# Feed-forward of a two-model block: one 512-column matmul for the high and low data against the high weights

## The reference

```python
for l in range(DEPTH):                                  # DEPTH = 2
    h = rms_norm(x, attn_norm_g[l])
    ...                                                 # three mixers on h @ w_in[l]
    x = x + jnp.concatenate([ya, yb, yc], axis=-1) @ w_out[l]
    h = rms_norm(x, ffn_norm_g[l])
    x = x + (jax.nn.silu(h @ ffn_w_gate[l]) * (h @ ffn_w_up[l])) @ ffn_w_down[l]
return rms_norm(x, final_norm_g)
```

## Time and profile before

| | |
|---|---|
| time, median of 3 runs | 940.64 us |
| lowest and highest | 939.58 and 940.69 us |
| span of the profiled execution | 938.7 us |
| time of the median run outside such a span | 1.9 us |
| mean granted clock of TensorE over the span | 0.997 |
| first feed-forward stage, PE | 147.2 to 327.6 us |
| second feed-forward stage, PE | 460.9 to 641.2 us |

### The profile page before, as it was taken

One profiled execution on the slowest core, in us unless ns is written; L12 is line 12 of the kernel. 1 busy time (PEld: TensorE's weight loads), 2 busy tenths in 40 slices (PEclk: granted clock), 3 DMA queues, 4 the chain that ended last, 5 costly groups with the idle time before them and its releaser, 6 DMA issues.

```text
span 938.7 us, 20423 instructions
## 1 busy us (share of the span) xinstructions
PE 916.4 (98%) x8848; PEld 869.5 (93%) x8848; DVE 680.7 (73%) x972; ACT 555.8 (59%) x851; POOL 7.6 (1%) x12
## 2 busy tenths in 40 slices
PE   8899999999999999999999999999999999999996
PEld 7788799999999999878999999999989899989896
DVE  6899667866664589976777666448799679588675
ACT  6873566654443588355754544338587667585665
POOL 0010000000000001000000000000000000000000
PEclk9999999999999999999999999999999999999998
DMA  8342115665554544211466655554544335444231
GB/s 324 151 174 95 48 56 188 214 261 183 201 201 180 180 163 151 98 64 46 140 251 232 250 192 182 204 197 135 179 136 138 132 135 180 147 168 157 93 135 67
DMA packets 24169, 150.94 MB, mean 161 GB/s; under 512 B 2960, under 2 KB 3472, under 8 KB 7056
## 3 DMA queue, kind: packets, MB, share of 16 engines
q1 hardware_dynamic: 24080, 149.64, 44.7%
HBM read 147.26 MB, written 1.05 MB: 158 GB/s over the span
## 4 chain that ended last, share of the span: by engine, by line
PE 67%; DVE 20%; ACT 7%; issue 3%; SPq 1%; DMA 1%; DVEq 0%; ACTq 0%
PE bank L1914 9%; PE bank L1912 8%; PE bank L1913 8%; DVE w_lo L277 6%; PE bank L2145 4%; PE bank L1936 3%; PE bank L1934 3%; PE bank L1935 3%; PE bank L2146 3%; PE bank L2147 3%; ACT w_hi L271 2%; PE bank L1075 1%; PE bank L2177 1%; PE bank L589 1%; PE bank L1165 1%
## 5 line engine op out<-in xcount | busy, mean ns | idle before, releaser
L277 DVE TENSOR_TENSOR w_lo<-w_raw,w_hi 128x1024 fp32r<-128x1024 f32 x256 | 306.0, 1224 | 106.2 <-ACT w_hi L271 105.5
L271 ACT ACTIVATE w_hi<-w_raw 128x1024 fp32r<-128x1024 f32 x256 | 259.4, 1054 | 206.3 <-PE bank L1914 104.9
L1912 PE MATMUL bank<-act_hi,w_hi 128*128 128x256 f32 x704 | 194.5, 276 | 0.0
L1913 PE MATMUL bank<-act_lo,w_hi 128*128 128x256 f32 x704 | 194.3, 276 | 0.0
L1914 PE MATMUL bank<-act_hi,w_lo 128*128 128x256 f32 x704 | 194.3, 276 | 0.0
L1912 PEld LDWEIGHTS bank<-act_hi,w_hi 128*128 128x128 f32 x704 | 132.2, 188 | 0.1
L1913 PEld LDWEIGHTS bank<-act_lo,w_hi 128*128 128x128 f32 x704 | 132.2, 188 | 0.0
L1914 PEld LDWEIGHTS bank<-act_hi,w_lo 128*128 128x128 f32 x704 | 132.2, 188 | 0.0
L2145 PE MATMUL bank<-act_hi,w_hi 128*128 128x256 f32 x352 | 100.2, 285 | 0.3
L2147 PE MATMUL bank<-act_hi,w_lo 128*128 128x256 f32 x352 | 97.7, 278 | 0.0
L2146 PE MATMUL bank<-act_lo,w_hi 128*128 128x256 f32 x352 | 97.7, 278 | 0.0
(11 more groups left out here) (367 smaller groups left out, 1982.1 us busy)
## 6 DMA issues: line engine op xcount, KB each, us to landing
w_raw<-in_w_ffn SPq DMA_DIRECT2D x66, 1024.0 KB, 4.8
w_raw<-in_w_mix SPq DMA_DIRECT2D x62, 1024.0 KB, 4.9
small_w<-in_small SPq DMA_DIRECT2D x2, 1280.0 KB, 7.6
w_raw<-in_w_mix SPq DMA_DIRECT2D x8, 256.0 KB, 6.3
x_res<-in_x_channels SPq DMA_DIRECT2D x4, 256.0 KB, 6.1
probs<-in_w_mix SPq DMA_DIRECT2D x2, 512.0 KB, 7.5
probsT<-in_w_mix SPq DMA_DIRECT2D x1, 1024.0 KB, 10.1
mem<-in_mem_channels SPq DMA_DIRECT2D x1, 1024.0 KB, 7.2
```

What stands on the lines that cost most here:

```text
L271: self.nc.scalar.activation(hi, self.piece(self.raw_slot(g), p), ACT.Copy).then_inc(self.hi_ready, 1)
L277: self.nc.vector.tensor_tensor(lo, self.piece(self.raw_slot(g), p), hi.bitcast(fp32), ALU.subtract).then_inc(self.lo_ready, 1)
L1912: TE.matmul(o, hi[:, w], HI[:, k, :], start=(k == 0 and x == 0), stop=False)
L1913: TE.matmul(o, hi[:, w], LO[:, k, :], start=False, stop=False)
```

## The change

Gate and up chunks 6 to 21 and all down chunks get a new form. `HI` and `LO` become two halves of one tile `HL`, and `GHI` and `GLO` of `GHL`. The high weights meet both in one matmul of 512 columns, whose moving operand is 256 columns of the high and 256 of the low data. It fills a whole bank: half h = 0 holds high times high, half h = 1 holds high times low. The matmul of low weights and high data adds into half 1. An output tile thus takes a bank of its own, and its two halves are added when they are taken out: for gate and up, ACT copies half 1 of two banks (`gate_rest`, `up_rest`), DVE adds half 0 and multiplies by the norm's row in a second operation; for down, `x_add_halves` adds one half to `X` after the other. Chunks 0 to 5 keep the old form.

Since eight down outputs now take all eight banks, and the gate/up chunks still use some of them at first, the down weights are cut anew (`DOWN_TILES`): a first pass over all 22 k tiles for outputs 0 to 3, in banks 4 to 7, and a second for outputs 4 to 7, in banks 0 to 3. There are 16 blocks a chunk as before. The adds of the first four outputs stand in the middle of the down part, and at the stage's end the split of chunk N+1 moves ahead of `lo(3)`. Semaphore names of the final norm also change ("turned"), with no change to its work.

```diff
+DOWN_TILES = [(k, o) for h in (0, 4) for k, o in
+              [(k, h + x) for k in range(FK - 4) for x in range(4)] + [(k, h + x) for x in range(4) for k in range(FK - 4, FK)]]
...
-        self.HI = self.sb("act_hi", [P, KT, T], f32r)
-        self.LO = self.sb("act_lo", [P, KT, T], f32r)
+        self.HL = self.sb("act", [P, 2, KT, T], f32r)
+        self.HI, self.LO = self.HL[:, 0, :, :], self.HL[:, 1, :, :]
...
+        if self.down and p in (0, 3):
+            eng.wait_ge(self.K.st.chunk_used, self.chunk - (0 if p else 6))
+        elif self.down:
+            eng.wait_ge(self.K.sem("out_done"), 2 * (self.n - 1) + p)
+        elif p % 2:
             eng.wait_ge(self.K.st.chunk_used, self.chunk - 1 + p // 2)
         else:
             eng.wait_ge(self.K.sem("out_done"), 2 * (self.n - 1) + p // 2 + 1)
...
+    def x_add_halves(self, dve, ch, p, halves):
+        x = self.K.X[:, 2 * p:2 * p + 2, :]
+        self.wait_out(dve, p)
+        ch(self.nc.vector.tensor_tensor(x, x, halves[:, :, 0, :], ALU.add))
+        self.nc.vector.tensor_tensor(x, x, halves[:, :, 1, :], ALU.add).then_inc(self.K.sem("x_new"), 1)
...
+    def first_bank(i):
+        return (4, 6, 0, 2)[(i - WIDE) % 4]
+    def halves(n):
+        return K.PS[:, 512 * n:512 * (n + 2)].rearrange("p (j h t) -> p j h t", j=2, h=2)
...
+    def wide_part(pe, i, p):
...
         hi, lo = st.slot(i)
...
+        if p == 0 and i < WIDE + 4:
+            pe.wait_ge(*at("gate_used", (1, 2, 3, 3)[i - WIDE]))
+            pe.wait_ge(*at("up_used", (1, 2, 2, 3)[i - WIDE]))
+        elif p == 0:
+            pe.wait_ge(*at("up_used" if i % 2 else "gate_used", (i - 4) // 2 + 1))
         if p % 2 == 0:
             st.arrived(pe, i, p // 2)
-        if i == LAST and p == 0:
-            pe.wait_ge(*at("gated_lo", NB))
-        elif i < LAST and p == 0:
-            pe.wait_ge(*at("gated_lo", i - DOWN + 1))
-        for x, (k, o) in enumerate(steps):
-            w = slice((4 * p + x) * P, (4 * p + x + 1) * P)
-            out = banks[o // 2][:, (o % 2) * T:(o % 2 + 1) * T]
-            TE.matmul(out, hi[:, w], GHI[:, k, :], start=(k == 0 and o % 2 == 0), stop=False)
-            TE.matmul(out, hi[:, w], GLO[:, k, :], start=False, stop=False)
-            last = TE.matmul(out, lo[:, w], GHI[:, k, :], start=False, stop=(k == FK - 1 and o % 2 == 1))
+        for k in (2 * p, 2 * p + 1):
+            for x in range(2):
+                bank, w = banks[first_bank(i) + x], slice(k * T + x * P, k * T + (x + 1) * P)
+                TE.matmul(two(bank), hi[:, w], HL[:, :, k, :], start=(k == 0), stop=False)
+                last = TE.matmul(bank[:, T:2 * T], lo[:, w], HI[:, k, :], start=False, stop=(k == KT - 1))
         if p == 3:
             last.then_inc(st.chunk_used, 1)
-        elif i >= LAST and p == 1:
...
+    def down_bank(o):
+        return banks[(o + 4) % 8]
+    def down_part(pe, i, p):
+        hi, lo = st.slot(i)
+        if p % 2 == 0:
+            st.arrived(pe, i, p // 2)
+        if i == DOWN and p == 0:
+            pe.wait_ge(*at("gate_used", NB - 1))
+            pe.wait_ge(*at("up_used", NB - 1))
+        for x in range(4 * p, 4 * p + 4):
+            k, o = DOWN_TILES[16 * (i - DOWN) + x]
+            if o == 0 and k % 2 == 0:
+                pe.wait_ge(*at("gated_lo", k // 2 + 1))
+            w, bank = slice(x * P, (x + 1) * P), down_bank(o)
+            TE.matmul(two(bank), hi[:, w], GHL[:, :, k, :], start=(k == 0), stop=False)
+            last = TE.matmul(bank[:, T:2 * T], lo[:, w], GHI[:, k, :], start=False, stop=(k == FK - 1))
+        if p == 3:
+            last.then_inc(st.chunk_used, 1)
+        elif p == 1 and i in (DOWN + 5, N - 1):
             last.then_inc(sem("out_done"), 1)
...
+    def x_add(dve, ch, p):
+        after.x_add_halves(dve, ch, p, halves((4, 6, 0, 2)[p]))
...
+    def gate_rest(act, b):
+        st.used(act, 2 * b + 1)
+        act.wait_ge(*at("gate_used", b))
+        S.activation(GATE_REST[:, :, :], halves(first_bank(2 * b))[:, :, 1, :], ACT.Copy).then_inc(*up("rest_sb"))
...
+    def gate_sb(dve, ch, b):
         if b:
             dve.wait_ge(*at("gated", b))
-        V.tensor_tensor(GATE[:, :, :], two(bank_of(2 * b)[:, :]), RSB2, ALU.mult).then_inc(*up("gate_used"))
+        if b < B0:
+            st.used(dve, 2 * b + 1)
+            V.tensor_tensor(GATE[:, :, :], two(bank_of(2 * b)[:, :]), RSB2, ALU.mult).then_inc(*up("gate_used"))
+        else:
+            dve.wait_ge(*at("rest_sb", 2 * (b - B0) + 1))
+            ch(V.tensor_tensor(GATE[:, :, :], halves(first_bank(2 * b))[:, :, 0, :], GATE_REST[:, :, :], ALU.add))
+            V.tensor_tensor(GATE[:, :, :], GATE[:, :, :], RSB2, ALU.mult).then_inc(*up("gate_used"))
...
     def up_sb(dve, ch, b):
-        st.used(dve, 2 * b + 2)
-        ch(V.tensor_tensor(UPS[:, :, :], two(bank_of(2 * b + 1)[:, :]), RSB2, ALU.mult), "up_used")
+        if b < B0:
+            st.used(dve, 2 * b + 2)
+            ch(V.tensor_tensor(UPS[:, :, :], two(bank_of(2 * b + 1)[:, :]), RSB2, ALU.mult), "up_used")
+        else:
+            dve.wait_ge(*at("rest_sb", 2 * (b - B0) + 2))
+            ch(V.tensor_tensor(UPS[:, :, :], halves(first_bank(2 * b + 1))[:, :, 0, :], UP_REST[:, :, :], ALU.add))
+            ch(V.tensor_tensor(UPS[:, :, :], UPS[:, :, :], RSB2, ALU.mult), "up_used")
...
     def _(pe):
-        for p in range(4):
-            proj_part(pe, 0, p)
-        for i in range(1, DOWN):
+        for i in range(WIDE):
             for p in range(4):
                 proj_part(pe, i, p)
             if i == 2:
                 norm.spread(pe, banks[0])
                 settle(pe)
         norm.wait_rs(pe)
+        for i in range(WIDE, DOWN):
+            for p in range(4):
+                wide_part(pe, i, p)
         for i in range(DOWN, N):
             for p in range(4):
                 down_part(pe, i, p)
...
+            if 7 <= i <= DOWN:
+                if i % 2 == 1:
+                    gate_rest(act, i // 2)
+                elif i >= 8:
+                    up_rest(act, i // 2 - 1)
             st.split_hi(act, i + 1, 0)
             st.split_hi(act, i + 1, 1)
...
-        after.hi(act, 0)
-        after.squares(act, 0)
-        if layer == 1:
-            after.scaled_squares(act, 0)
+            elif i == DOWN + 6:
+                after.hi(act, 0)
+                after.hi(act, 1)
+            elif i == DOWN + 7:
+                after.squares(act, 0)
+                after.squares(act, 1)
+            elif i == DOWN + 8 and layer == 1:
+                after.scaled_squares(act, 0)
+                after.scaled_squares(act, 1)
         st.split_hi(act, N, 0)
-        after.hi(act, 1)
         st.split_hi(act, N, 1)
         after.hi(act, 2)
-        after.squares(act, 1)
         after.squares(act, 2)
+        st.split_hi(act, N + 1, 0)
         after.hi(act, 3)
         after.squares(act, 3)
-        st.split_hi(act, N + 1, 0)
-        if layer == 1:
-            after.scaled_squares(act, 1)
...
-        after.x_add(dve, 0, banks[0])
-        after.lo(dve, 0)
-        after.x_add(dve, 1, banks[1])
+            elif i == DOWN + 5:
+                x_add(dve, ch, 0)
+            elif i == DOWN + 6:
+                x_add(dve, ch, 1)
+            elif i == DOWN + 7:
+                after.lo(dve, 0)
+                after.lo(dve, 1)
+            elif i == DOWN + 8:
+                after.square_sum(dve, 1)
         st.split_lo(dve, N, 0)
-        after.lo(dve, 1)
-        after.x_add(dve, 2, banks[2])
+        x_add(dve, ch, 2)
         st.split_lo(dve, N, 1)
         after.lo(dve, 2)
-        after.x_add(dve, 3, banks[3])
-        after.square_sum(dve, 1)
+        x_add(dve, ch, 3)
+        st.split_lo(dve, N + 1, 0)
         after.lo(dve, 3)
         after.square_sum(dve, 2)
         after.square_sum(dve, 3)
```

More of the change, by code:

```diff
@@ L189, in __init__ @@
         raw = K.sb("w_raw", [P, 2, CHUNK], top=True)
-        hi, lo = (K.sb(f"w_{x}", [P, 2, CHUNK], f32r, top=True) for x in ("hi", "lo"))
+        self.w = K.sb("w_split", [P, 2, 2, CHUNK], f32r, top=True)
+        lo, hi = self.w[:, 0, :, :], self.w[:, 1, :, :]
         self.raw = [raw[:, i, :] for i in range(2)]
@@ L346, with __init__ @@
 class Norm:
-    def __init__(self, K, n, chunk, gain):
-        self.K, self.nc, self.n, self.chunk, self.gain = K, K.nc, n, chunk, gain
+    def __init__(self, K, n, chunk, gain, down=False):
+        self.K, self.nc, self.n, self.chunk, self.gain, self.down = K, K.nc, n, chunk, gain, down
     def wait_out(self, eng, p):
-        if p % 2:
+        if self.down and p in (0, 3):
[3 more added lines that the diff above has]
+        elif p % 2:
             eng.wait_ge(self.K.st.chunk_used, self.chunk - 1 + p // 2)
@@ L432, in __init__ @@
     def __init__(self, K, n, chunk, gain, g1, SQ2, R1):
-        super().__init__(K, n, chunk, gain)
+        super().__init__(K, n, chunk, gain, down=True)
         self.g1, self.SQ2, self.R1 = g1, SQ2, R1
@@ L1884, in stage_ffn @@
```

(38 more changed lines are left out.)

15 lines of the change are left out of this document (4 added, 11 removed).

## The result

The changed kernel takes 950.78 us (median of 4 runs, 950.23 to 952.50) against 940.50 us before. The ratio is 1.0115 with a 95% interval of 1.0102 to 1.0127: slower by 10.3 us, where 8.7 us faster was forecast.

A forecast was written before the change was run, and what follows sets the result against it. It took TensorE issuing matmuls back to back in the feed-forward stages as the bound. Span 938.7 - 9.5 (matmul pace) + 0.8 (stage ends) = 930.0 us; with 1.9 us from span to median, 931.9 us, range 927.2 to 936.7.

The forecast's parts named there:

- What bounds the kernel: Feed-forward stages: bound by TensorE issuing matmuls one behind another; DVE and ACT matter only if they outgrow that pace.
- What the 6.6 ns are: Wide chunks: 113.3 ns is the weight load's pace, so a 512-column matmul costs 215.7 ns; 9.5 us won over 864 triples.
- D: Rival, wide chunks: extra goes with the columns, 226.7 ns for 512, triple stays 340 ns; 941.4 us, chance 0.08.
- The other term: Wide chunks: the 256-column matmul after the long one costs 113.3 ns, making 329.0 ns a triple.
- B: Rival, wide chunks: extra stays with each matmul, or slower 256-column pace; about 333 ns a triple, 935.5 us, chance 0.18.
- E: Rival, wide chunks: the break in the moving operand makes the 512-column matmul 233.3 ns; 947.1 us, chance 0.04.
- C: Rival, wide chunks: both weight loads vanish behind streaming, 325 ns a triple; gain 13.0 us, 928.4 us, chance 0.08.
- DVE, ACT and transfers: Wide chunks: added copies and adds cost nothing; DVE busy rises 28 us, ACT 19 us; a chunk lasts 5.26 us.
- New waits on PE: Wide chunks and down tiles: PE's new waits for data finished chunks ago cost nothing.
- The stage ends: Ends of both feed-forward stages: 0.8 us lost, between -0.4 and 2.0; in its times E marks PE's down work ending.

The follow-up runs named there:

- e5: Kernel before plus a block of thrown-away matmuls, 24 in a row of each width and type (split type and bf16); 979.81 us in one run.
- e8: Kernel before plus another thrown-away block of split-type matmuls, varying weights, adding up and width, a settle between sequences; 988.89 us in one run.
- e3: Changed kernel without the 256-column matmuls of the wide chunks (low weights times high data), leaving only 512-column ones; 889.76 us in one run.
- e9: Changed kernel without the settle transpose behind the spread in both feed-forward stages; 952.56 us, ratio 1.0135.
- e10: Changed kernel's two-bank layout with each 512-column matmul as two of 256, and without the settle transpose behind the spread; 952.66 us, ratio 1.0138.
- e2: Changed kernel with high and low data of a tile side by side, so the 512-column moving operand is one contiguous run; 951.17 us, ratio 1.0118.
- e1: Changed kernel with each 512-column matmul split into two of 256 into the same halves, all else kept; 940.43 us, ratio 1.0004 to the kernel before.
- e7: Kernel before without the settle transpose behind the spread in both feed-forward stages; 951.54 us, ratio 1.0122.
- e6: Kernel before with the rearrangement alone: down in two passes, first four adds under the down matmuls, all matmuls 256 columns; 938.89 us, ratio 0.9990.

## Why the prediction was wrong

**What bounds the kernel** was right: PE without a hole in the wide chunks of both stages before and after, and all of the loss is in its pace.

**The failed step** is "What the 6.6 ns are". It took 215.7 ns for the 512-column matmul from a plain-float row and read 113.3 ns as the pace of the weight load. The 512-column matmul costs 235.0 ns in the changed kernel. In a row of its like it settles at 226.7 (e5, e8) or 233 ns (e3), and no single one of the split type came under 224 in any run; with only one load in 233 ns it still has 20 ns besides streaming (e3). What a matmul of this type carries besides its streaming is not what plain float or bf16 carries, and the trace of before had no long one of the type. The type's own matmul of half the length was nearer than rows 7: twice its 113.3 ns is 226.7, which gives D and at least no gain. The rest of the loss is the pace: against triples at the slow pace the new form costs nothing (e9, e10), and what it loses is the fast pace, which no pair of a long and a short one kept in any run.

**The other term**, 113.3 ns for the 256-column one, was 118.3. The slow pace of the earlier trace rows stood among the rivals as a side case of B, with a 512-column matmul of 215.7. It is what happened, to both (235.0 is twice 117.5): 13.3 ns a pair lost (353.3 against 340.0) and not 11.0 won. That the engine has two paces for one and the same triple could be seen in the earlier trace rows. The prediction speaks of nine matmuls in a row at the slower one, where the trace has 94; it priced that pace for the short matmul alone and did not ask what the new form would settle at.

**Rivals.** E gave 346.6 ns a pair and 947.1 us, nearest to what came, but for a reason that e2 refutes. D (columns) named 226.7 ns for the long one, which is where a row of long ones settles (e5, e8), but the surcharge does not grow with the columns (e5) and the pair never got there. C is the price in bf16 (e5), not here.

**DVE, ACT and transfers** cost nothing, as said: e1 has all of their work and the old time. DVE rose by 25.5 us (28 foreseen), ACT by 17.8 (19). DVE's work in a chunk went as laid out, though the chunk lasts 16 x 0.3533 = 5.65 us and not 5.26; for an odd chunk in DVE's timeline:

```profile
209.43 0.69 DVE L2009 TENSOR_TENSOR gate<-bank,gate_rest 128x512 f32<-128x512 f32 x1 [0.71 <-ACT gate_rest L1994]
210.16 0.69 DVE L2010 TENSOR_TENSOR gate<-gate,norm_rs 128x512 f32<-128x512 f32 x1
210.77 2.35 DVE L281 TENSOR_TENSOR w_split<-w_raw,w_split 128x1024 fp32r<-128x1024 f32 x2
```

**New waits on PE** cost nothing: PE stands in no wait of the wide chunks.

**The stage ends** went nearly as laid out, step by step. The square sum was ready at E+5.9 and not E+6.4 (E = 332.8), PE waited 0.3 us for it and not 1, and the spread went at 338.78. The reciprocal came at 340.54, E+7.7, where 8.1 was forecast and 7.6 stood before. The first two rows are of DVE's timeline, the last is of the list of waits:

```profile
338.30 0.42 DVE L417 TENSOR_TENSOR squares<-squares 128x256 f32<-128x256 f32 x1
...
340.54 1.77 DVE L435 RECIPROCAL norm_rs<-norm_rs 128x258 f32<-128x258 f32 x1 [0.39 <-ACT norm_rs L430]
...
PEld bank L425 <- DVE squares L417: 0.3, 1, 0.3
```

What the stage ends are worth in all is not shown by this profile. The parts between and behind the stages got 1.8 us shorter in it, where 0.8 us longer was forecast. But 0.8 us of that is pace. Behind the spread of the mixer after each feed-forward stage, 94 starts at 117.8 ns became starts at 113.3; two rows of PE's timeline in the changed kernel, nine starts apart (1.02 us):

```profile
341.70 0.28 PE L1154 MATMUL bank<-act,w_split 128*128 128x256 f32 x1
...
342.72 0.28 PE L1154 MATMUL bank<-act,w_split 128*128 128x256 f32 x1
```

And the two parts together differ by 1.0 us among the four profiles in which their code is the old one (before, e5, e7, e8: 429.7 to 430.7 us; the changed kernel 428.9). The best measure of the term is e1, which has all of the rearrangement and the old pace in the stages: 0.0004 over the kernel before, 0.4 us, with -0.6 to 1.2 left open. That holds the 0.8 us of the forecast, and nothing as well.

**What stays open.** Why the split type has several settled paces (113.3, 117.8 and 120 ns at 256 columns; 226.7 and 233.3 ns for rows of 512) and what decides between them. The runs show only that the pace changes at a disturbance, that rows of equal matmuls keep it, and that a long and a short one in turn always settled at 353.3 ns a pair. The place of the weight load inside a matmul, which may be behind it, can't be seen in these records.

## What to carry to other kernels

Merging matmuls saves only what a matmul costs besides its streaming, here 6.6 of 113.3 ns, so before building on it measure the long one in the same type, in the same alternation, in a row of some twenty. Read the pace from starts at every seam of the timeline: a stage can run some 4% slower for its whole length because of what stood in front of it, with every busy share at 100%. If a large change of form moves the time, split it at once into the form alone and the layout alone; here the layout was free, and the two passes cost nothing and may win a microsecond (e6).

## What the runs showed of the hardware that was not expected

- Matmuls of the split type have more than one settled pace for the same work: 113.3, 117.8 or 120.0 ns for 256 columns at clock 1.00. Taking away one transpose a stage (0.27 us in the profile) put both stages on 117.8 ns: 12.5 us more in the two stages, 11.5 us more in the time (e7).
- The same instructions can leave either pace behind them. At the spread of the mixer behind the first stage, the second one-column matmul starts 26 ns behind the first before and 133 ns behind it in the changed kernel, where PE had waited 0.3 us; the starts behind it are the same within 1 ns up to the second matmul of the split type. From there on the pace is 117.8 ns in the one and 113.3 in the other. A wait ahead does not always bring the fast pace: in the second stage of the changed kernel a break of 0.2 us was followed by 117.8 ns.
- Every settled mean of the split type is a whole multiple of 6.67 ns, that is of 16 cycles at 2.4 GHz: 113.3, 120.0, 146.7, 173.3, 226.7 and 233.3 ns for one matmul, 340.0 and 353.3 ns for a triple or pair (117.8 ns is a third of 353.3). It holds for the unit that repeats and not for each start in it (118, 235, 226 or 231 ns stand in such rows), and bf16 (109 and 216 ns) does not follow it.
- The surcharge of the split type over its streaming, in settled rows, is 6.6 to 13.3 ns at 256 columns (before, e5), and at 512 it is 13.3 ns in a row of equal ones and 21.7 ns in the pair of the changed kernel (e5, after), against 2 to 3 ns in bf16.
